# Cached pages of a hybrid decoder step: two softmax maps in one partition, half as many transposes, keys in two bursts

## What is computed

```python
s = einsum('bqhd,bkhd->bhqk', q, k) * DH**-0.5 + bias[bucket(q_pos - k_pos)]   # 16 maps: 2 per head
p = softmax(s, axis=-1).reshape(b, 2, DA_HEADS, lq, lk)
pd = p[:, 0] - lam * p[:, 1]                                    # the two maps of a head
o  = einsum('bhqk,bkhv->bqhv', pd, v)                           # 2048 cached keys + 8 new ones
S_new = decay * S_old + kd^T v                                  # per sample and head, 128 x 128
```

## Time and profile before

| | |
|---|---|
| median of 3 runs | 1887.02 us (1885.8 to 1888.24) |
| the profiled execution, whole | 1886.7 us |
| its span in the profile | 1885.1 us |
| PE busy | 1872.3 us (99%) |
| DVE busy | 1047.3 us (56%) |
| ACT busy | 820.3 us (44%) |
| POOL busy | 111.1 us (6%) |
| DMA packets | 444.27 MB, mean 236 GB/s |

### The profile page before, as it was taken

The page is one execution under the profiler, slowest core; times in us unless marked ns, Lnnn a source line. Parts: engine busy times, 40 slices in busy tenths (PEclk is TensorE's granted clock), DMA queues, the critical chain, the costliest instruction groups (busy, mean ns, idle before and its releaser), DMA issues.

```text
span 1885.1 us, 38230 instructions
## 1 busy us (share of the span) xinstructions
PE 1872.3 (99%) x14710; PEld 1775.3 (94%) x14710; DVE 1047.3 (56%) x1393; ACT 820.3 (44%) x1075; POOL 111.1 (6%) x135
## 2 busy tenths in 40 slices
PE   9999999999999999999999999999999999999998
PEld 9999888888888888799999999999999999999998
DVE  8443656656565566575547754544554445545555
ACT  6333444435544355454445433333333334445454
POOL 1001021010210111100000000000000000000000
PEclk9999999999999999999999999999999999999999
DMA  8877999999999999977544444445444454544441
GB/s 316 180 257 258 329 360 338 380 352 353 365 340 377 354 357 367 336 280 251 189 149 153 163 162 160 150 157 178 156 166 151 154 174 157 166 157 157 167 156 57
DMA packets 123998, 444.27 MB, mean 236 GB/s; under 512 B 14581, under 2 KB 18693, under 8 KB 123872
## 3 DMA queue, kind: packets, MB, share of 16 engines
q1 hardware_dynamic: 112720, 402.31, 59.7%
q0 software_dynamic: 9984, 39.63, 7.1%
q10 hardware_dynamic: 1232, 1.47, 0.2%
HBM read 423.43 MB, written 22.54 MB: 237 GB/s over the span
## 4 chain that ended last, share of the span: by engine, by line
PE 96%; DVE 2%; DMA 2%; issue 0%; POOL 0%; ACT 0%; DVEq 0%; SPq 0%; POOLq 0%; ACTq 0%
PE ps L449 50%; PE ps L438 6%; PE ps L439 6%; PE ps L440 6%; PE ps L1860 5%; PE ps L1861 5%; PE ps L1862 5%; PE ps L953 3%; PE ps L1502 3%; PE ps L981 2%; PE ps L962 1%; DMA raw<-w_in 1%; DMA gates<-uT 0%; DMA raw<-w_hg 0%; PE ps L755 0%
## 5 line engine op out<-in xcount | busy, mean ns | idle before, releaser
L374 DVE TENSOR_TENSOR w_lo<-raw,w_hi 128x1024 fp32r<-128x1024 f32 x416 | 506.4, 1230 | 502.2 <-ACT w_hi L369 243.4
L369 ACT ACTIVATE w_hi<-raw 128x1024 fp32r<-128x1024 f32 x236 | 246.6, 1058 | 366.6 <-PE ps L449 301.6
L1860 PE MATMUL ps<-hid_hi,w_hi 128*128 128x320 f32 x680 | 203.4, 299 | 0.0
L1862 PE MATMUL ps<-hid_lo,w_hi 128*128 128x320 f32 x680 | 203.3, 299 | 0.0
L1861 PE MATMUL ps<-hid_hi,w_lo 128*128 128x320 f32 x680 | 203.3, 299 | 0.0
L449 PE MATMUL ps<-x_hi,w_hi 128*128 128x320 f32 x1200 | 190.9, 303 | 0.0
L397 ACT ACTIVATE w_hi<-raw 128x1024 fp32r<-128x1024 f32 x124 | 129.9, 1053 | 135.8 <-DMA raw<-w_in 112.1
L449 PEld LDWEIGHTS ps<-x_hi,w_hi 128*128 128x128 f32 x1200 | 169.3, 189 | 10.8 <-issue 8.3
L449 PE MATMUL ps<-x_hi,w_lo 128*128 128x320 f32 x1136 | 177.5, 299 | 0.0
L449 PE MATMUL ps<-x_lo,w_hi 128*128 128x320 f32 x1072 | 167.5, 299 | 0.0
L449 PEld LDWEIGHTS ps<-x_hi,w_lo 128*128 128x128 f32 x1136 | 161.9, 189 | 0.0
(11 more groups left out here) (360 smaller groups left out, 3083.0 us busy)
## 6 DMA issues: line engine op xcount, KB each, us to landing
raw<-w_in SPq DMA_DIRECT2D x176, 512.0 KB, 7.7
raw<-w_up SPq DMA_DIRECT2D x176, 512.0 KB, 3.5
raw<-ck SPq DMA_DIRECT2D x128, 512.0 KB, 6.3
raw<-cv SPq DMA_DIRECT2D x128, 512.0 KB, 6.9
raw<-w_dn SPq DMA_DIRECT2D x88, 512.0 KB, 3.5
raw<-w_out SPq DMA_DIRECT2D x32, 512.0 KB, 4.4
uT<-stage POOLq DMA_DIRECT2D x14, 640.0 KB, 4.2
raw<-w_hg SPq DMA_DIRECT2D x16, 512.0 KB, 4.7
```

The lines of the kernel that those rows point to most:

```text
L369: act.activation(w_hi[slot % HALVES][:, :], raw[slot][:, :], ACT.Copy).then_inc(hi_ready, 1)
L374: dve.tensor_tensor(w_lo[half][:, :], raw[slot][:, :], w_hi[half][:, :].bitcast(F32), ALU.subtract).then_inc(lo_ready, 1)
L1860: pe.matmul(ps[:, m, 0:T], wh[:, c], xh, **dict(add, start=q == 0))
L1862: ins = pe.matmul(ps[:, m, 0:T], wh[:, c], xl, **dict(add, stop=q >= 3))
```

## The change

- The cached keys' scores are laid out anew. A column tile of 32 partitions (j) holds two heads by two halves of the pages (pages 0 to 7, and 8 to 15 with the new keys) by 8 queries; the two maps lie side by side in the free dimension (`s_all[:, m, :]`, 2 x 1032), in PSUM banks 5 and 7. A product takes the 64 partitions of one map, so a row tile of 64 by a column tile of 32; there are 32 for a burst of eight pages.
- The keys come in two bursts of eight pages, after A1 and after A5. Before burst 1 PE waits for `pdt`, the ACT copy out of bank 5, which ACT makes behind the split of A6; `o_s0` moves ahead of burst 1, and the copy `i_smp` behind `pdt`.
- The maxima and sums are exchanged between the two halves by `stream_shuffle`; DVE combines the maps (`differ`: reciprocal, scaling, one subtraction over 1032 columns), then PE turns 8 pages and the new keys. `w_row`, `coef` and `o_second` go.
- On DVE the last maximum (`most`, with `near`) moves from behind the split of D2 to ahead of that of D0, the new state (L682) to behind the read-out after D0, and `differ` stands behind the split of D1. On ACT the exponentials move from behind D2 to behind D0.
- The states' sums are four products of 32 rows by 256 columns in four row tiles (banks 4 to 7).
- `near` and `far` are loaded in 40 transfers where there were 2, ahead of the store of the new values as before.

```diff
-ROUND = (items("A", 0, 1) + items("K", 0, 4) + items("A", 1, 4) + items("K", 4, 8) + items("A", 4, 6)
-         + items("K", 8, 12) + items("A", 6, 8) + items("K", 12, 16) + items("D", 0, 4) + items("V", 0, 8)
-         + items("D", 4, 7) + items("V", 8, 16) + items("D", 7, 8))
+BURSTS = [[("K", i) for i in (*range(4 * g, 4 * g + 4), *range(8 + 4 * g, 12 + 4 * g))] for g in range(2)]
+ROUND = (items("A", 0, 2) + BURSTS[0] + items("A", 2, 6) + BURSTS[1] + items("A", 6, 8) + items("D", 0, 4)
+         + items("V", 0, 8) + items("D", 4, 7) + items("V", 8, 16) + items("D", 7, 8))
...
             if q == 6:
-                act.wait_ge(h_pe.sem, h_pe.at(h, "o_s0"))
-                h_act.done(act.activation(i_tok[:, 2, :], ps[:, 6, 2 * P:3 * P], ACT.Copy), "i_smp")
                 act.wait_ge(h_pe.sem, h_pe.at(h, "pd_t"))
                 h_act.done(act.activation(pdt[:, :, :], ps[:, 5, 0:3 * P].rearrange("p (c d) -> p c d", c=3),
                                           ACT.Copy), "pdt")
+                act.wait_ge(h_pe.sem, h_pe.at(h, "o_s0"))
+                h_act.done(act.activation(i_tok[:, 2, :], ps[:, 6, 2 * P:3 * P], ACT.Copy), "i_smp")
...
-                for b in range(2):
-                    t = slice(CHUNK * b, CHUNK * b + CHUNK)
-                    ins = pe.matmul(ps[:, 6 - b, :], kd_tok[t, 2, :], i_own[t, :, :], start=True, stop=True)
+                pe.wait_ge(h_vec.sem, h_vec.at(h, "o"))
+                pe.wait_ge(k_vec.sem, k_vec.at(h, "near"))
+                for j in range(4):
+                    t = slice(32 * j, 32 * j + 32)
+                    ins = pe.matmul(ps[:, 4 + j, 0:2 * DV], kd_tok[t, 2, :], i_own[t, :, :], start=True, stop=True)
...
+            elif what == "differ":
+                dve.wait_ge(k_act.sem, k_act.at(r, "p"))
+                chain(dve.stream_shuffle(l_all[:, 1, :], l_all[:, 0, :], OTHER_HALF), "l")
...
+                chain(dve.tensor_scalar(s_all[:, 1, :], s_all[:, 1, :], l_all[:, 2, 1:2], None, ALU.mult), "pd2")
+                k_vec.done(dve.scalar_tensor_tensor(s_all[:, 0, :], s_all[:, 0, :], l_all[:, 3, 0:1], s_all[:, 1, :],
+                                                    ALU.mult, ALU.add), "pd")
...
         def scores(pe, r, g):
-            for p in range(QUAD * g, QUAD * g + QUAD):
-                pe.wait_ge(*landed(r, ("K", p)))
+            for kind, p in BURSTS[g]:
+                pe.wait_ge(*landed(r, (kind, p)))
             if g:
-                pe.wait_ge(k_act.sem, k_act.at(r, f"g{g - 1}"))
-            at = ring_of(r).slot["K", QUAD * g]
-            for e in range(2):
-                for j in range(4):
-                    h = 2 * j + e
-                    ins = pe.matmul(ps[32 * j:32 * j + 32, 7, :], q_rows[:, h, :],
-                                    raw_all[:, at:at + QUAD, h * PAGE:(h + 1) * PAGE], start=e == 0, stop=e == 1)
-            k_pe.done(ins, f"s{g}")
+                pe.wait_ge(k_act.sem, k_act.at(r, "g0"))
+                pe.wait_ge(h_act.sem, h_act.at(r, "pdt"))
+            else:
+                pe.wait_ge(h_vec.sem, h_vec.at(r, "s"))
+            for half in range(2):
+                at = ring_of(r).slot["K", 8 * half + QUAD * g]
+                for e in range(2):
+                    for j in range(4):
+                        for m in range(2):
+                            h, own = 2 * j + e, slice(DH * m, DH * m + DH)
+                            ins = pe.matmul(ps[32 * j:32 * j + 32, MAP_BANK[m], :], q_rows[own, h, own_rows(half, e)],
+                                            raw_all[own, at:at + QUAD, h * PAGE:(h + 1) * PAGE],
+                                            start=half == 0 and e == 0, stop=half == 1 and e == 1)
+                k_pe.done(ins, f"{'hs'[half]}{g}")
         def turn(pe, r):
-            pe.wait_ge(k_act.sem, k_act.at(r, "p"))
-            pe.wait_ge(h_vec.sem, h_vec.last(r))
-            for t in range(PAGES):
-                ins = pe.transpose(ps[:, (6, 7, 4, 5)[t // 4], t % 4 * P:(t % 4 + 1) * P],
-                                   s_all[:, t * PAGE:(t + 1) * PAGE], ident[:, :])
+            pe.wait_ge(k_vec.sem, k_vec.at(r, "pd"))
+            pe.wait_ge(h_vec.sem, h_vec.at(r, "s_three"))
+            for t in range(PAGES // 2):
+                pe.transpose(ps[:, 4 + t // 4, t % 4 * P:(t % 4 + 1) * P], s_all[:, 0, t * PAGE:(t + 1) * PAGE], ident[:, :])
+            v_pe.done(pe.transpose(ps[0:NQ, 7, 0:P], s_all[:, 0, HALF:], ident[:, :]), "pt")
...
-            pool.dma_start(near[:, :], bass.AP(bias_rows.tensor, P - 1, rows + [[BIAS_L - 1, NQ], [1, NEAR]])).then_inc(mix_landed, 16)
-            pool.dma_start(far[:, :], bass.AP(bias_rows.tensor, 0, rows + [[BIAS_L, NQ], [1, 2]])).then_inc(mix_landed, 16)
+            for j in range(4):
+                first, last = slice(32 * j, 32 * j + 16), slice(32 * j + 16, 32 * j + 32)
+                for m in range(2):
+                    row = (4 * j + m) * P * BIAS_L
+                    two = [2 * P * BIAS_L, 2]
+                    for dst, at, step, n in ((near[last, m, :], P - 1, BIAS_L - 1, NEAR), (near[first, m, 0:PAGE], 0, BIAS_L, PAGE),
+                                             (near[first, m, PAGE:], 2 * P, BIAS_L, NQ), (far[first, m, :], 0, BIAS_L, 2),
+                                             (far[last, m, :], 0, BIAS_L, 2)):
+                        pool.dma_start(dst, bass.AP(bias_rows.tensor, row + at, [two, [step, NQ], [1, n]])).then_inc(mix_landed, 16)
```

More of the change, by code:

```diff
@@ L45 @@
 QUAD = 4
+HALF = PAST // 2
+OTHER_HALF = [i ^ 16 for i in range(32)]
 SETS_IN, SETS_U, FIRST = 22, 6, 7
@@ L302, in build @@
         s0_landed = sem("s0_landed")
-        h_pe = Steps(sem("h_pe"), "vk scores i_t kd_t a o_s0 ds pd_t pv o ds_s", 1)
-        h_act = Steps(sem("h_act"), "ef tok lg eG p i_tok kd_tok i_smp pdt o_att", 1)
-        h_vec = Steps(sem("h_vec"), "i_smp fg kin s max nmax G Gd qk qkd rc rcl pd2 pd aT st1 mid st2 own o s_new", 1)
+        h_pe = Steps(sem("h_pe"), "vk scores i_t kd_t a ds pd_t o_s0 pv o ds_s", 1)
+        h_act = Steps(sem("h_act"), "ef tok lg eG p i_tok kd_tok pdt i_smp o_att", 1)
+        h_vec = Steps(sem("h_vec"), "i_smp fg kin s max nmax G Gd qk qkd rc rcl pd2 pd aT st1 mid st2 own o s_three s_new", 1)
         passed = sem("passed")
@@ L312, in build @@
         v_n_landed = sem("v_n_landed")
-        k_pe = Steps(sem("k_pe"), "new s0 s1 s2 s3", 1)
+        k_pe = Steps(sem("k_pe"), "new h0 s0 h1 s1", 1)
         k_pool = Steps(sem("k_pool"), "zero ss", 1)
-        k_act = Steps(sem("k_act"), "q silu g0 g1 g2 g3 p sq rt rt_da", 1)
-        k_vec = Steps(sem("k_vec"), "new silu m0 m1 m2 near m3 mx nmx r w rs on og rs_da da", 1)
-        v_pe = Steps(sem("v_pe"), "pt pn new ot", 1)
-        v_act = Steps(sem("v_act"), "p0 pn o ot", 1)
+        k_act = Steps(sem("k_act"), "q silu g0 g1 p sq rt rt_da", 1)
+        k_vec = Steps(sem("k_vec"), "new silu m0 near m1 mx other most nmx l sum r w pd2 pd rs on og rs_da da", 1)
+        v_pe = Steps(sem("v_pe"), "pt new ot", 1)
+        v_act = Steps(sem("v_act"), "p0 pn o", 1)
         v_vec = Steps(sem("v_vec"), "p1 o", 1)
@@ L893, in vec_pages @@
                 dve.wait_ge(k_pe.sem, k_pe.at(r, "new"))
-                k_vec.done(dve.tensor_tensor(s_all[:, PAST:], ps[:, 4, 3 * P:3 * P + NQ], near[:, PAGE:], ALU.add), "new")
+                k_vec.done(dve.tensor_tensor(s_all[:, :, HALF:], ps[:, 4:6, 3 * P:3 * P + NQ], near[:, :, PAGE:], ALU.add), "new")
             elif what == "silu":
@@ new lines, in turn, with values @@
+        def turn(pe, r):
+            pe.wait_ge(k_vec.sem, k_vec.at(r, "pd"))
+            pe.wait_ge(h_vec.sem, h_vec.at(r, "s_three"))
+            pe.sem_inc(passed, 1)
+            for t in range(PAGES // 2):
+                pe.transpose(ps[:, 4 + t // 4, t % 4 * P:(t % 4 + 1) * P], s_all[:, 0, t * PAGE:(t + 1) * PAGE], ident[:, :])
+            v_pe.done(pe.transpose(ps[0:NQ, 7, 0:P], s_all[:, 0, HALF:], ident[:, :]), "pt")
+        def values(pe, r, half):
+            if half == 0:
+                pe.wait_ge(h_vec.sem, h_vec.last(r))
+                pe.wait_ge(v_act.sem, v_act.at(r, "p0"))
+                pe.wait_ge(v_vec.sem, v_vec.at(r, "p1"))
+            else:
+                pe.wait_ge(v_act.sem, v_act.at(r, "pn"))
+                pe.wait_ge(v_n_landed, 16 * r + 16)
+            pe.sem_inc(passed, 1)
+            for p in range(PAGES // 2 * half, PAGES // 2 * (half + 1)):
@@ L1032, in act_last @@
             act_gates(act, r)
-            for q in range(2):
-                round_hi(act, r, "D", q)
-            for what in ("g3", "p", "sq", "p0"):
-                act_pages(act, r, what)
+            round_hi(act, r, "D", 0)
+            round_hi(act, r, "D", 1)
+            act_pages(act, r, "p")
+            act_pages(act, r, "sq")
             round_hi(act, r, "D", 2)
+            act_pages(act, r, "p0")
             act_pages(act, r, "pn")
```

237 lines of the change are left out of this document (102 added, 135 removed).

## The result

The changed kernel takes 1907.9 us (median; 1906.2 to 1909.1) where the kernel before takes 1886.7: a ratio of 1.0111, 95% interval 1.0093 to 1.0128. The forecast had the right sign, but 1895.2 us, and the time is 4.5 us above the high end of its range. The profiled execution has a span of 1907.5 us against 1885.1.

The account below looks back on a forecast made before the run. PE bounds the kernel (99% busy), with DMA hardly behind. 1886.7 us plus entry 8.0, round 0 -1.2, rounds 1 to 6 +2.8 and last round -1.1 gives 1895.2 us; range 1883.5 to 1903.4.

Parts of the forecast that it names:

- PE work per round, -1.24: PE work in each round: turning saves 0.93 us, scores 0.2, state sums 0.46; new keys' scores lose 0.35; 1.24 less.
- What must stay covered: DVE and ACT beside PE in each round: `differ`, 4 us, lies under 9.8 us of PE work, at no cost.
- Burst 1 behind `pdt`: Second burst each round: PE waits 1.7 us for copy `pdt` behind late A6; round 77.9 against 77.44, 0.46 more.
- The entry, +8.0: Start of kernel: 40 bias loads on POOL idle PE 6.3 us, once, and slow clock behind adds 1.7 us.
- Round 0, -1.2: First round: keys have time to land during the wait at the entry, so PE has its gain, 1.2 us less.
- The last round, -1.1: Last round: `ds_s` and new state come sooner, one ACT copy goes, burst 1 later as before: 1.1 us less.
- `ds_s` and the new state come sooner: Last round: both come some 3 us sooner, part of the 1.1 us less forecast there.
- Range: Whole kernel: 1883.5 to 1903.4 us; high end takes 1.3 us more in six rounds and clock loss of 2.8.
- held longer or the queue starves: Store of new values held beyond the issues, or queue starves behind late slots of burst 1: above 1904 us; 8%.
- PE alone (1876.9): Rival: PE alone sets the time in entry and rounds, nothing it waits for moves behind it: 1876.9 us; 8%.

Follow-up runs that it names:

- 9: Changed kernel with GpSimd's wait for the store of the gate set moved behind the sum over the partitions in every round: 1914.7 us.
- 3: Changed kernel with both ACT copies written ahead of a split, `v_tok` ahead of that of A2 and `pdt` ahead of that of A6: 1892.9 us.
- 5: Changed kernel with the copy `v_tok` alone ahead of the split of A2, `pdt` staying behind the split of A6: 1903.1 us.
- 6: Changed kernel with each value page's transfer cut to its first half of columns, the second half left out of the attention: 1904.4 us.
- 7: Changed kernel with transfers reordered: A2 and A3 ahead of burst 0's second four keys, A6 ahead of burst 1's second four: 1898.9 us.
- 1: Changed kernel with its 40 bias loads issued ten by ten between the stores of round 0's sets: 1898.7 us.
- 10: Changed kernel with GpSimd's wait for the store of the gate set moved behind the sum over the partitions in the last round alone: 1903.2 us.
- experiment 11: Changed kernel with all three edits (bias loads spread, `v_tok` and `pdt` ahead of splits, GpSimd's store wait behind the sum in the last round): 1879.3 us, ratio 0.9969.
- experiment 2: Kernel before with its two bias loads cut into 40 of the same bytes at the same place: 1891.2 us, ratio 1.0028.

## Why the prediction was right and wrong, by its own steps

- **PE work per round, -1.24.** Right as a sum, in part by luck. With the waits gone a round takes 76.28 us against 77.44: -1.16. By pieces: turning 257.23 to 258.13, 0.90 (forecast 0.94); a burst 3.60 (3.55), so the row tiles do work side by side; state sums 0.65 (0.6). Wrong was the new keys' scores: 0.27 instead of the forecast 0.70, less than the 0.35 of 16 instructions before. I priced them by the instruction, and the price of one fell from 0.022 to 0.008 us; whether by the second row tile or by the 64 rows is not told apart. The four pieces together are 1.56 less; 0.2 of waiting at the burst and 0.2 between the pieces, which I had not, brought the sum back to the forecast.
- **What must stay covered.** Right: DVE's `differ` made PE wait in no steady round (it takes 2.84 us, forecast 4). That its cover is thin showed only when GpSimd was put beside it (9).
- **Burst 1 behind `pdt`.** The number was right (77.79 measured, 77.9 forecast; A6 split at 48.95 instead of 49.7 after the values), but half by luck: a wait that was too large and one that was left out made up for each other. The waits of PE from 340 to 715 us, nearly five rounds of the kernel after, are shared between two places:

```profile
PE ps L971 <- ACT pd L586: 3.1, 5, 1.7
PE ps L719 <- ACT v_tok L562: 2.4, 3, 0.9
PE ps L971 <- issue: 1.5, 4, 0.4
PE ps L971 <- DVE nmx L637: 0.4, 1, 0.4
```

The first is 0.6 us a round at the second burst, where I had 1.7, and 0.2 of it stays with `pdt` early (3). The other three seem to belong together: PE waits at L719 for `v_tok` behind A2, and the rows of 0.4 us are at the first burst right behind, and go when that copy is moved (5). They make 0.9 us a round, which I had not. I asked this question of the sixth granule and not of the second, which had moved in the queue in the same way; the earlier trace rows would have been worth reading for A2 too. With A2's copy out of the way (5) the wait at the burst is 1.4 us and the round 77.45. And the lateness was priced as bytes at the queue's rate, 1.46 us for each of four transfers. Halving the values' bytes moved neither granule (6), and four keys fewer ahead of it moved A2 by 5.8 and A6 by 5.2 us (7). What counts in these rounds is when PE frees the first slot of a burst, and from there 1.2 us for each key that SP has to issue. That the landings behind a burst are 1.28 us apart makes the two prices nearly equal here, so that the forecast came out near does not show which of them holds for A6.
- **The entry, +8.0.** Right for the gap: 5.07 us (5.9), PE there at 202.28 (202.6), slow clock behind it 1.6 (1.7). The 1.7 was picked between 0 and 2.8 with nothing to choose by, so that it fits is luck. (The clock of the first 6 us is not to be read in the earlier trace rows, whose line has one digit for 47 us.) Taken away, the forty loads gave 9.2.
- **Round 0, -1.2.** Failed, +5.9 in its place (of the 13.1 by which the values start later, 5.6 are PE's arrival at the new keys and 1.6 the clock behind it; 4.3 of the rest is the wait for `pdt`, 2.3 the clock behind that). I had the keys land during the entry's wait. The keys of burst 1 can't: their slots are held by those of burst 0, which PE reads only at 208.54. They were issued from 210.74 on, beside the head's loads and behind the two big output copies that the forty loads had pushed from 185 to 202 us, and A6 took 12.0 us from issue to split where it takes 6.7 in a steady round. That the output copies are what slows it is an inference from the times; with the copies back in their place (1) the largest wait for `pdt` was 2.5 us instead of 4.3, with the gap ahead of it gone too, so the two are not told apart. In the executions of 5, 9 and 10, whose entry is that of the change, this wait was 2.6 to 3.1, so much of the difference is between executions.
- **The last round, -1.1.** Failed: +9.1 up to the turn back. About 3 of them lie ahead of its values and come from the late copies, as in the rounds (77.4 us from values to values, 74.3 with the copies moved), and 6.0 behind them, which GpSimd's wait costs (20.6 us, 14.6 without it). The change by itself moves 2.3 us of the stretch to ahead of the values: it is 72.0 and 16.9 in the kernel before, 74.3 and 14.3 with all three edits. I followed the norm's chain by its engines and not by the queue that feeds it. GpSimd stands in that chain behind a wait for a store. GpSimd by time in the last round, the kernel before and then the one after:

```profile
775.39 0.77 POOL L787 DMA_DIRECT2D uT<-stage  x1 [30.78 <-DVE stage L547]
781.22 0.55 POOL L795 DMA_DIRECT2D h_p<-state  x1 [5.06 <-DVE s L682]
...
782.64 0.97 POOL L1173 MEMSET v_new<- 128x1024 f32 x1
```

```profile
796.15 0.78 POOL L788 DMA_DIRECT2D uT<-stage  x1 [37.11 <-DVE stage L545]
798.54 0.94 POOL L796 DMA_DIRECT2D h_p<-state  x1 [1.62 <-DVE s L680]
...
804.33 0.95 POOL L1176 MEMSET v_new<- 128x1024 f32 x1 [3.96 <-DMA uT<-stage]
```

Before, the store was down when the state was ready; now the state comes 2.4 us behind the store's issue, and the store lands in 8.0 us instead of 4.6, so the wait is on the path. "`ds_s` and the new state come sooner" was true against the store, and worth nothing: with all three edits the last round is 0.3 us under the kernel before (88.7 against 88.9), not 1.1. Why the store is slower is seen in the load of the DMA engines while it is under way, in the kernel before and then in the one after (columns as above):

```profile
775.40:780.00 4.60, 4.32 (x32) 3.29 (x24) 4.50 (x14) 2.03 (x2) 0.76 (x1) 1.00 0.72 204
796.15:804.20 8.05, 8.05 (x63) 8.03 (x63) 6.20 (x16) 3.33 (x6) 2.60 (x3) 1.00 1.01 373
```

Before, the engines had time left beside it; now they are full with values and granules. With half of their bytes (6) the share is 0.57 and it lands in 3.7 us. The order on GpSimd makes the lateness count (10).
- **Range.** The high end left out both failed steps, 7.1 us in round 0 and 10.2 in the last. The rival that named something of the kind ("held longer or the queue starves", above 1904) had a chance of 8% and no working.
- **PE alone (1876.9).** What this rival described is what experiment 11 made, with a span of 1876.6, by three edits outside the change.

## What to carry to other kernels

When transfers are put in another order, ask for every item that moved back, not for the one that moved furthest, which copies are written behind its use, and price its lateness by when the queue may issue it (the slot that is waited for, and the issues ahead) before its bytes. Work that depends on no transfer should be written ahead of an instruction that waits for one. And where an engine gets its result sooner, look at what its neighbour waits for next in program order: a wait for a store that was always long down can be the new path, and moving it can put two engines side by side that slow each other (9).

## What the runs showed of the hardware that was not expected

- 32 matmul instructions of 64 rows by 32 columns of weights with 8 moving columns start over 0.27 us; 16 of 128 rows took 0.35.
- Pages of keys are issued 1.16 to 1.28 us apart by SyncE's queue, also where their slots are free, value pages 0.4 to 0.6.
- Gaps of PE of 5.07, 4.33 and 6.49 us (and of 3.22 in experiment 2) were each followed by some microseconds at the lower clock (0.68, 0.70 and 0.58 on average over 6 to 7 us), 1.6 to 2.5 us lost each time, little depending on the gap. Waits under 2 us can bring it too (1.85 us in 9, 1.43 and 0.39 in 10), where most such waits in these traces did not. The Trainium skill ("TensorE: Matmul & The Clock Gate", Part 1) says that the slower level is the default; all of these stretches agree.
- The same store of 640 KB lands in 4.2 us (median) in the kernel before and in 8.0 in the one after, at nearly the same bytes per round: while the last of them was under way the DMA engines were busy for 0.72 and for 1.01 of the time. With half of the values' bytes it lands in 3.7.
- A memset of 0.97 us on GpSimd made a step of DVE 1.0 us longer (0.81 to 1.81), and a sum over the partitions of 3.92 us cost three splits 2.2 us.
